# Two edits of the instruction order in a hybrid decoder kernel: the transpose of the mLSTM output one chunk later, and other PSUM banks in the short convolution

## What is computed

```
layer 0 mixer: mLSTM, 4 heads, dqk 128, dv 256
  num = (q k^T * Dm) v + sc * q C          den likewise with n
  hs  = num / max(|den|, exp(-m))          C = decay*C + sum w k v^T
  hs  = rmsnorm_per_head(hs) * sigmoid(o)  out = hs @ w_out
layer 1 mixer: short convolution
  b, c, xin = split(x @ w_in)              out = (b * conv3(c * xin)) @ w_out
after each mixer: ConvFFN, d_ff 2816
  gate, val = split(conv3(x @ w_up))       out = (silu(gate) * val) @ w_down
```

## Time and profile before

| what | value |
|---|---|
| median of three runs | 2046.3 us (2042.81 to 2047.39) |
| the profiled execution | 2045.24 us |
| its span, slowest core (core 4) | 2043.7 us |
| spans of the eight cores | 2034.0 to 2043.7 us |
| mean granted TensorE clock | 0.910 to 0.921 |
| TensorE busy, matmuls | 1738.7 us, 85% |
| VectorE busy | 1301.4 us, 64% |
| ScalarE busy | 818.6 us, 40% |
| GpSimd busy | 311.1 us, 15% |
| chain that ended last | TensorE 64%, VectorE 14%, ScalarE 10%, issue 7% of the span |

### The profile page before, as it was taken

One profiled execution on the slowest core, in us unless ns is written; L12 is line 12 of the kernel. 1 busy time (PEld: TensorE's weight loads), 2 busy tenths in 40 slices (PEclk: granted clock), 3 DMA queues, 4 the chain that ended last, 5 costly groups with the idle time before them and its releaser, 6 DMA issues.

```text
span 2043.7 us, 31133 instructions; the slowest of 8 cores (2034.0 to 2043.7 us)
## 1 busy us (share of the span) xinstructions
PE 1738.7 (85%) x9528; PEld 896.6 (44%) x9580; DVE 1301.4 (64%) x2384; ACT 818.6 (40%) x1577; POOL 311.1 (15%) x333
## 2 busy tenths in 40 slices
PE   2678677878787699999999969888869999999993
PEld 0233344343433255555555524444425555555550
DVE  2344435353434688888888865555568888888885
ACT  1222354344544544444444452111154444444444
POOL 1210201010000022222222200000002222222220
PEclk9788888888998699999999969989969999999995
DMA  9911000000005500404030090014050040404004
GB/s 209 212 43 42 1 1 1 1 1 1 1 1 78 78 1 1 63 1 63 6 58 1 11 155 1 1 18 61 0 78 1 1 63 1 63 2 62 1 1 165
DMA packets 54242, 79.08 MB, mean 39 GB/s; under 512 B 1984, under 2 KB 33088, under 8 KB 54080
## 3 DMA queue, kind: packets, MB, share of 16 engines
q0 software_dynamic: 40272, 51.56, 17.3%
q1 hardware_dynamic: 13808, 25.52, 4.0%
HBM read 120.25 MB, written 8.39 MB: 63 GB/s over the span
## 4 chain that ended last, share of the span: by engine, by line
PE 64%; DVE 14%; ACT 10%; issue 7%; DMA 2%; another core or an unknown queue 2%; DVEq 1%; POOL 1%; ACTq 0%; POOLq 0%
PE B L240 63%; ACT SCF L253 6%; DVE CX L265 4%; ACT SCB L253 3%; DVE SCF L265 3%; DVE X L256 2%; DMA RA<-l_w_in 2%; DVE SCF L256 1%; PE B L243 1%; DVE SCB L256 1%; DVE CX L260 1%; DVEq L155 1%; DVE X L265 1%; POOL SCB L503 0%
## 5 line engine op out<-in xcount | busy, mean ns | idle before, releaser
L240 PE MATMUL B<-CX,RA 128*128 128x413 bf16 (+3 forms) x5107 | 932.0, 344 | 21.6 <-DVE CX L256 11.3
L240 PEld LDWEIGHTS B<-CX,RA 128*128 128x128 bf16 x5120 | 501.6, 99 | 439.1 <-issue 38.5
L265 DVE SCALAR_TENSOR_TENSOR SCF<-B,vecs,SCF 128x411 f32<-128x411 f32 (+1 forms) x880 | 557.0, 645 | 112.5 <-ACT SCF L253 52.3
L253 ACT ACTIVATE SCF<-B,vecs 128x411 f32<-128x411 f32 (+1 forms) x440 | 302.3, 691 | 452.2 <-PE B L240 448.7
L240 PE MATMUL B<-SCB,RA 128*128 128x411 bf16 (+1 forms) x2080 | 395.7, 346 | 35.8 <-DVE X L256 35.4
L256 DVE TENSOR_TENSOR X<-X,B 128x411 f32<-128x411 f32 (+3 forms) x520 | 303.4, 583 | 120.3 <-PE B L240 81.4
L818 POOL TENSOR_TENSOR SCB<-SCB,SCF 128x411 bf16<-128x411 bf16 (+1 forms) x220 | 213.6, 971 | 741.1 <-DVE SCF L265 616.9
L240 PEld LDWEIGHTS B<-SCB,RA 128*128 128x128 bf16 x2080 | 198.8, 100 | 223.8 <-issue 93.3
L240 PE MATMUL B<-RA,CX 128*128 128x512 bf16 (+1 forms) x1122 | 261.6, 375 | 40.8 <-DVE CX L265 15.7
L253 ACT ACTIVATE SCB<-SCF 128x411 bf16<-128x411 f32 (+3 forms) x284 | 157.2, 564 | 122.4 <-DVE SCF L265 91.1
L265 DVE SCALAR_TENSOR_TENSOR CX<-X,vecs,SCF 128x411 bf16<-128x411 f32 (+5 forms) x192 | 128.6, 670 | 108.1 <-ACT SCF L253 92.6
(11 more groups left out here) (40 smaller groups left out, 570.6 us busy)
## 6 DMA issues: line engine op xcount, KB each, us to landing
RA<-l_w_up POOLq DMA_DIRECT2D x12, 1024.0 KB, 14.8
RA<-l_w_up POOLq DMA_DIRECT2D x8, 1280.0 KB, 17.3
RA<-l_w_in POOLq DMA_DIRECT2D x8, 1024.0 KB, 28.3
X<-xm SPq DMA_DIRECT2D x4, 2048.0 KB, 27.4
y<-X SPq DMA_DIRECT2D x4, 2048.0 KB, 6.9
X<-xp SPq DMA_DIRECT2D x3, 2048.0 KB, 25.7
RA<-l_w_down POOLq DMA_DIRECT2D x6, 1024.0 KB, 22.2
RA<-l_w_down POOLq DMA_DIRECT2D x4, 1280.0 KB, 27.2
```

Source lines behind the costliest of these rows:

```text
L240: P.add("pe", lambda e: e.matmul(out, lhsT=lhsT, rhs=rhs, start=start, stop=stop), reads, writes)
L253: P.add("act", lambda e: e.activation(out=out, in_=in_, func=func, **kw), reads, writes)
L265: P.add("dve", lambda e: e.scalar_tensor_tensor(out=out, in0=in0, scalar=scalar, in1=in1, op0=op0, op1=op1), reads, writes)
```

## The change

B_hT can be told to use bank 3. The loop no longer calls B_hT(i) at the end of iteration i for a full chunk that is neither the last of its group nor the last of all: it keeps the number, and calls B_hT(i) in iteration i+1, behind A_gates and A_qk "q" and ahead of B_T(i+1). In the last chunk of a group B_hT stays where it was. This concerns 12 chunks: 16 to 18, 20 to 22, 24 to 26 and 28 to 30.

In the short convolution a block takes banks 4 (b), 0 or 1 (c) and 2 or 3 (xin), and the parts are computed in the order c, xin, b. down() takes banks 5, 6, 7 in turn.

The FFN gets two more SBUF buffers, tp1, and a branch that would do one convolution tap on ScalarE and GpSimd; it is behind a switch that is off by default, so that the FFN issues the instructions that it issued before.

```diff
-        def B_hT(i):
+        B3bf = banks[3][:].bitcast(BF16)
+
+        def B_hT(i, late=False):
...
+            pb_, pk_ = (B3bf, "B3") if late else (B5bf, "B5")
             for vb in range(8):
-                TR(B5bf[:, vb * 128:(vb + 1) * 128], hst[par][:, vb * 128:(vb + 1) * 128], ["hst%d_%d" % (par, vb // 2)], ["B5"])
-            TT(hsT[:, :, cs:cs + 128], v3(B5bf[:, 0:1024], 8), ogT[:, :, cs:cs + 128], ALU.mult, ["B5", "ogT"], ["hsT"])
+                TR(pb_[:, vb * 128:(vb + 1) * 128], hst[par][:, vb * 128:(vb + 1) * 128], ["hst%d_%d" % (par, vb // 2)], [pk_])
+            TT(hsT[:, :, cs:cs + 128], v3(pb_[:, 0:1024], 8), ogT[:, :, cs:cs + 128], ALU.mult, [pk_, "ogT"], ["hsT"])
...
                 A_gates(nx)
                 A_qk(nx, "q")
+            if late_hT[0] is not None:
+                B_hT(late_hT[0], late=True)
+                late_hT[0] = None
             if ch["full"]:
                 B_T(i)
...
             if ch["full"]:
-                B_hT(i)
-                if ch["last"]:
-                    do_wout(ch["g"])
+                if ch["last"] or nx is None or not LATE_HT:
+                    B_hT(i)
+                    if ch["last"]:
+                        do_wout(ch["g"])
+                else:
+                    late_hT[0] = i
...
-            dnb = [4, 5, 6, 7] if kind == "ffn" else [6, 7]
+            dnb = [4, 5, 6, 7] if kind == "ffn" else [5, 6, 7]
...
-                    bks = [upb[par * nparts + q] for q in range(nparts)]
-                    for q in range(nparts):
+                    if kind == "ffn":
+                        bks = [upb[par * nparts + q] for q in range(nparts)]
+                        qorder = range(nparts)
+                    else:
+                        bks = [4, par, 2 + par]
+                        qorder = (1, 2, 0)
+                    for q in qorder:
                         for kc in range(KC):
...
+                            if USE_ACT_TAP:
+                                t1_ = tp1[q][:, 0:no]
...
+                            else:
+                                STT(outs[q][:, 0:no], pb[:, 1:n - 1], wc(1), outs[q][:, 0:no], ALU.mult, ALU.add,
+                                    ["B%d" % bks[q], "vec", nm], [nm])
```

More of the change, by code:

```diff
@@ L643, in build_program @@
         carrier = {1: 1}
+        late_hT = [None]
+        LATE_HT = os.environ.get("K_LATEHT", "1") == "1"
         for G in range(2, len(groups)):
@@ L718, in proj_phase @@
                 sg = [bB.get(TW), bB.get(TW)]
+                tp1 = [bF.get(TW), bF.get(TW)]
                 NBMAX = 5
@@ L759, in load_w @@
                     return dict(parts=aps, down=d_ap, keys=sk, nb=nb, b0=b0)
-            return dict(kind=kind, layer=layer, grp=grp, H=H, load_w=load_w, gstate=gstate,
+            return dict(kind=kind, layer=layer, grp=grp, H=H, load_w=load_w, gstate=gstate, tp1=(tp1 if kind == "ffn" else None),
                         bufs=(ag, av, sg) if kind == "ffn" else (tc_, cx, yy))
@@ L765, in build_program @@
         USE_POOL_H = os.environ.get("K_POOLH", "1") == "1"
+        USE_ACT_TAP = os.environ.get("K_ACTTAP", "0") == "1"
         def run_proj(ph, preloaded=None):
@@ L801, in up @@
                         ag, av, sg = ph["bufs"]
+                        tp1 = ph["tp1"]
                         base = V_FC + layer * 176
@@ L810, in up @@
                             ACT(outs[q][:, 0:no], pb[:, 2:n], AF.Identity, ["B%d" % bks[q], "vec"], [nm], scale=wc(2), bias=bc)
-                            STT(outs[q][:, 0:no], pb[:, 1:n - 1], wc(1), outs[q][:, 0:no], ALU.mult, ALU.add,
-                                ["B%d" % bks[q], "vec", nm], [nm])
+                            if USE_ACT_TAP:
+                                t1_ = tp1[q][:, 0:no]
+                                o_ = outs[q][:, 0:no]
+                                ACT(t1_, pb[:, 1:n - 1], AF.Identity, ["B%d" % bks[q], "vec"], ["tp1_%d" % q], scale=wc(1))
+                                P.add("pool", lambda e, o_=o_, t1_=t1_: e.tensor_tensor(out=o_, in0=o_, in1=t1_, op=ALU.add),
+                                      [nm, "tp1_%d" % q], [nm])
+                            else:
+                                STT(outs[q][:, 0:no], pb[:, 1:n - 1], wc(1), outs[q][:, 0:no], ALU.mult, ALU.add,
+                                    ["B%d" % bks[q], "vec", nm], [nm])
                             STT(outs[q][:, 0:no], pb[:, 0:n - 2], wc(0), outs[q][:, 0:no], ALU.mult, ALU.add,
```

## The result

The changed kernel takes 2008.91 us (median of 10 runs) beside 2045.2 us for the kernel before (10 runs); the ratio is 0.9815, with a 95% interval of 0.9802 to 0.9827. Two of the ten runs of the changed kernel were in the chip's slower state (2160.54 and 2209.53 us); they are in the median, but not in the ratio. That is 36 to 38 us less, where 55 was forecast. The profiled execution took 2008.68 us, with a span of 2007.1 us on its slowest core (core 6).

What follows compares the result with a forecast made beforehand. The prediction took TensorE as the bound, through its standstills and half-clock stretches. Gains of 20 + 34.3 + 4 - 3 = 55 us off 2045.24 gave 1990, own range 1980 to 1999 (chance 0.62), wide range 1979 to 2011.

Steps and rivals of the forecast that it cites:

- Rival 1: In both stages the clock still falls behind the shorter idles: 2007 us, chance 0.14.
- Rival 2: mLSTM seam wins nothing, as ScalarE's and VectorE's loop is the bound and hid the fallen clock: 2010 us, chance 0.08.
- down(), 34.3 forecast: Short convolution, eight down() steps followed by an up(): 6.6 us each, 52.8 against 87.1 us, 11.9 of the gain from clock.
- The single bank, nothing forecast: Short convolution, bank 4 for b: 24 products, 4.24 us, cover its 4.0 us chain, so no cost over 40 blocks.
- Rivals 3 and 4: Short convolution's bank 4 binds mildly: 2002 us, chance 0.09; or binds in each block, slower than before: 2070, chance 0.04.
- The start, -3 forecast: Start of the short convolution: only 40 products have banks, not 48; 1.4 us lost, perhaps a clock fall of 1.7.
- The mLSTM seam, 20 forecast: Twelve mLSTM chunk seams: gates and q fill TensorE's wait, so qkT starts earlier; 16.0 us plus 3.9 from B_S.
- One of the twelve subtractions, 1.8: At each mLSTM seam, qkT's start before less its floor; the twelve sum to 16.0 us, the fourth being 1.8.
- The floor of 4.12: mLSTM seams: ScalarE's copy qkT can't start before 4.12 us behind the Identity row; later at three seams with norm work.

Runs made afterwards that it cites:

- e3: Kernel before with only the short convolution's part order changed to c, xin, b, its banks and the mLSTM as before: 2015.78 us, ratio 0.9877.
- e4: Kernel before with only the short convolution's new banks, parts in the old order b, c, xin, mLSTM as before: 2199.81 us, ratio 1.0778.
- e9: e5 with the gates ahead of q again, q keeping its free bank 3: ratio 0.9764 to the kernel before.
- e11: Changed kernel plus products that nobody reads, in TensorE's idle time ahead of the gates at ten seams: 1992.19 us, ratio 0.9752.
- e5: Changed kernel with q in free bank 3 ahead of the gates, and other mLSTM banks reassigned: 1992.02 us, ratio 0.9743 to the kernel before.
- e1: Kernel before with only the mLSTM edit, short convolution as before: 2037.79 us, ratio 0.9977.
- e2: Kernel before with only the short-convolution edit, B_hT staying at the end of its iteration: 2006.08 us, ratio 0.9831.

## Why the prediction was right, and where its working failed

The time lies in the wide range of 1979 to 2011, near its upper end, and the direction was right. It doesn't lie in the forecast's own range of 1980 to 1999 but at the times of rivals 1 and 2 (2007 and 2010), and it is inside the wide range because that was drawn to take in rivals 1 to 3, not because the sum came out. Of the two large terms one was right and the other wrong by a factor of at least six. By the prediction's own mark for the mLSTM edit, chunks that shrink by less than 12 us, it was wrong there: they shrank by 3.1. The short convolution passed its mark of 25 with 36.7.

- **down(), 34.3 forecast, 33.7 measured** (87.1 less 53.4). Right in each step: 6.6 us per step (6.7 measured), idle 1.0 us (0.91), clock 1.0 in all eight windows, no wait in the blocks. e3 confirms that the earlier chain is what matters, with 1.6 us idle, 8.1 us a step and no clock fall.
- **The single bank, nothing forecast.** Right: 24 products cover the 4.0 us. e4 measured what the cover is worth. The Trainium skill's rule on rotating banks (Perfetto Trace Analysis, Optimizing Tensor Performance, Matmuls) would, read strictly as the prediction read it, have each block stall; this case's trace agrees with it only in e4's order, with 31 waits of 3.9 us, and not in the change's. Rivals 3 and 4 are out.
- **The start, -3 forecast.** Right: 3.20 us idle, where 1.53 was, and 152 products in 28.52 us, about 1.6 more than at 0.177 each.
- **The mLSTM seam, 20 forecast, 3 or less measured.** The step that failed: "In the place of the wait TensorE now does gates and q: it is free at 423.52". It was free, but gates and q were not: they write banks 0 and 1, where B_dC had left sums that VectorE reads after the Identity row has started. I followed the edit's own operands (hst, banks 3 and 5) and gave to gates and q, which moved ahead of a wait, no dependences of their own. Before, that wait on banks 0 and 1 lay hidden behind the transposes. The second part of the failure is the clock: with the idle kept, its fall was kept at most seams, and e9 and e11 show that this, not the idle, is most of the cost (in e9 the waits ahead of the gates are longer, and the stage is 13.5 us shorter). The prediction had gates and q done 0.3 us behind the start of the Identity row, 1.2 at the lower clock; at the seam of chunks 21 and 22 they were done 4.6 behind it. One of the twelve subtractions, 1.8, is also off by a little: by the same floor it is 6.15 less 4.12, 2.03.
- **The floor of 4.12.** Right: 4.00 in e5 and 4.3 in e11. The two later seams with norm work came to 5.55 and 5.78 (read in e1), where 5.8 and 6.0 had been worked out and 7.01 and 7.43 stood before. Here the edit did win something: TensorE's transposes waited for the norm's Ln, which reads bank 5, 3.5 us in 2 waits before, and B_hT in bank 3 has no such wait. The two seams together are 11.3 to 12.5 us on the cores of e1 and of the changed kernel, and 14.4 to 15.4 on those of the kernel before and of e2, e3 and e4. On the slowest cores that is 3.1 us, the first and the last of the twelve seams give 1.0, and the other eight give none.
- **Rival 2** gave the number, 2010, for the wrong reason: it said that the loop of ScalarE and VectorE was the bound and the clock hidden in it. e5 and e11 win 10 to 14 us in those chunks. That its number came out is luck.
- **Rival 1** was wrong for the short convolution and half right at the seams, where in the changed kernel the clock fell behind idles of 2.28 us or more, or had fallen shortly before the seam.

## What to carry to other kernels

When work is moved ahead of a wait to fill it, list the buffers that the moved-up work writes and who still reads them; a dependence that was hidden behind the old wait comes to light as the new one. When a buffer is given up, count the work between its last write and the next in its engine's order against the chain that frees it: 4.2 us of cover over 4.0 us of chain cost nothing, and no cover cost 158 us. When a wait's idle can't be removed, look at what runs behind it and at which clock, for that may be the larger part of its price.

## What the hardware showed that I had not expected

Products that nobody reads made the kernel about 13 us faster by the ratios (0.9752 beside 0.9815) and 10 us by the stage that they are in, because at the seams where they filled the idle the 8 products behind them ran at 2.4 GHz (1.9 us) and not at 1.2 GHz (3.2 us). The same idle of 2.28 us was followed by a fallen clock at one seam (0.65 from 425.0 to 428.4) and not at another (1.00 from 539.0 to 544.5) of one execution.
